# Hybrid decoder step: the sample batches' state products as pairs of 64-column strips of the array

## The chip, the cores and the metric

The kernel runs on one core of one Trainium2 chip. The metric is the device time of one execution in microseconds (us). The kernel before took 877.75 us, the median of three runs (877.45 to 877.9).

## The reference, cut to what matters

One decoder layer runs over 1024 prompt tokens and 8 sample batches of 8 tokens each: a combined projection, a pooling mixer beside a gated linear attention, an output projection, and a mixture of 16 experts. The change is in one output, the new attention state of the sample batches. For each batch b and head h (4 heads, 64 key and 128 value columns) the state is the decayed old state plus the sum over the batch's 8 tokens of key times value:

```python
S_new = jnp.exp(b_last[:, :, 0, :])[..., None] * S + jnp.einsum(
    'bhsk,bhsv->bhkv', ki * jnp.exp(b_last - bi), vi)
```

So 8 x 4 products of 64 x 128 are wanted, each over 8 tokens. The 64 sample tokens of all batches lie together on 64 partitions.

## The kernel before, in words

The program has three blocks, each ended by a barrier of all engines. `b1_all` computes the projections and the attention for the prompt and the samples. `b2_all` does the output projection, the residual, the second norm, the router, and the lists that say which rows go to which expert. `b3_all` walks through the experts, one step for each, with TensorE (PE) nearly always busy. In each block every engine has its own program, written out by hand, and works through it in that order; semaphores join them.

In `b1_all` the samples' decayed keys (`keys8`, 64 tokens x 256) and values (`v8`, 64 x 512) are left in SBUF, with `bmask` (64 x 8), which is 1 where a token belongs to a batch.

In `b2_all` the output projection goes through 9 row tiles (8 of 128 prompt rows, one of the 64 sample rows) and two column halves. The second half's loop (L1380 to L1404) has other work between its matmuls: after the third of the eight k it issues the transposes of the tile before (`turn`, L1351) and its router products (`logits`, L1377), later `partial_logits` (L1365). VectorE (DVE) has, for each tile i of that half, in this order (L1586 to L1605): the low parts of the next tile (`tile_lo`, L1545 and L1547), a router result (L1532), the reciprocal of the norm (L1594), the scaled row block `h2` = x times norm times weight (L1595, two whole operands from SBUF, 128 x 1024), the copy of the strip sums (`strips_out`, L1540), and the residual (L1563), which PE's next `turn` waits for.

GpSimd (POOL) waits until the last `tile_lo` has read the room `uT` (semaphore `r_al`, L1283). Then one multiply (L1284) writes `samples.masked` into that room: for each of the 8 batches the 256 keys of all 64 tokens, with the tokens of other batches set to zero. Its next instructions (L1287 on) wait for the router.

When the last sample tile is through, PE makes the state products (`states`, L1410). One batch b is two matmuls (L88), one for each pair p of heads: the masked keys of the pair (64 tokens x 128) are the weights and 256 value columns of the pair stream. That gives 128 x 256 in PSUM, of which two 64 x 128 blocks are wanted; the other two blocks pair one head's keys with the other head's values. ScalarE (ACT) takes the two wanted blocks out with two copies for each batch (`state_products_out`, L96) into `samples.added`, in the room `gT`. Each matmul has float32 operands and shows as two records in the trace, each with its own weight load. PE's order is: batches 0 to 2; the ranks (L1422 to L1428), for which it waits on DVE's choice of experts; batch 3; the lists of the first expert's rows, in two parts (L1438, c = 0 and 1), each after a DVE comparison (L1659); batches 4 to 7. From batch 4 on, a batch waits until its bank has been copied out. ACT copies batches 0 to 2, does two exponentials for the router, and copies batches 3 to 7. DVE meanwhile computes the choice of experts and the lists; after the first list (L1671 to L1675) POOL gathers the first expert's rows (L1297), and DVE goes on with the other lists and weights until L1700.

`samples.added` is read only in the last expert step (L2155), where DVE adds it to `S0`, the decayed old state.

`b3_all` begins on PE with reading the number of steps, the transposes of the gathered rows (L1900, L1905), the list products (L1893) and the gate and up matmuls (L1912).

Of the kernel before, what the change touches and what calls it, by code (L numbers as in the profile page):

```python
# [22 lines left out]
P = 128  # L23
# [3 lines left out]
DEC_B, DEC_T = 8, 8  # L27
NS = DEC_B * DEC_T
# [13 lines left out]
DK, DV = 64, 128  # L42
# [33 lines left out]
class Samples:  # L76


    def __init__(self, keys8, v8, o_dec, bmask, uT, gT):
        self.keys8, self.v8, self.o_dec, self.bmask = keys8, v8, o_dec, bmask  # L80
        self.masked = uT[0:NS, :, :].rearrange("p m t -> p (m t)")[:, 0:DEC_B * 256].rearrange("p (b d) -> p b d", b=DEC_B)
        self.added = gT[:].rearrange("p m t -> p (m t)")[:, 0:DEC_B * 2 * DV].rearrange("p (b q x) -> p b q x", b=DEC_B, q=2)


def state_products(nc, samples, bank, b, signal):

    for p in range(2):
        m = nc.tensor.matmul(bank[b % 4][:, p * 256:(p + 1) * 256], samples.masked[:, b, p * P:(p + 1) * P],  # L88
                             samples.v8[:, p * 256:(p + 1) * 256], start=True, stop=True)
    m.then_inc(signal, 1)  # L90


def state_products_out(nc, samples, bank, b, signal):

    for a in range(2):
        x = nc.scalar.copy(samples.added[64 * a:64 * a + 64, b, :, :],  # L96
                           bank[b % 4][64 * a:64 * a + 64, :].rearrange("p (q x) -> p q x", q=2)[:, :, a * DV:(a + 1) * DV])
    x.then_inc(signal, 1)

# [1095 lines left out]
def b2_all(nc, A, O, S0, Sp, s_w, samples, halves, sb, sem, e_w, wdn, bank, ident, onesf, eps_c, uT, gT, ring, x1, x_rows, h2_dram,  # L1195
# [41 lines left out]
    r_km, r_ku, r_us, r_ex = sem("r_km"), sem("r_ku"), sem("r_us"), sem("r_ex")  # L1237
# [15 lines left out]
    def _(pool):  # L1253
# [23 lines left out]
        for p in range(2):  # L1277
# [5 lines left out]
        pool.wait_ge(r_al, 2 * TT - 1 - PROJECTED)  # L1283
        nc.gpsimd.tensor_tensor(samples.masked, samples.keys8[:, :].unsqueeze(1).broadcast_to([NS, DEC_B, 256]),  # L1284
                                samples.bmask[:].unsqueeze(2).broadcast_to([NS, DEC_B, 256]), ALU.mult).then_inc(r_km, 1)
        pool.wait_ge(r_exd, 2)
# [56 lines left out]
    def _(pe):  # L1343
# [36 lines left out]
        for n in range(PROJECTED, 2 * TT):  # L1380
            h, i = n // TT, n % TT
# [6 lines left out]
            for k in range(KC):  # L1388
# [12 lines left out]
                m = nc.tensor.matmul(out, alo[:, s, k, 0:r], whi[:, k, :], start=False, stop=k == KC - 1)  # L1401
# [7 lines left out]

        def states(b):  # L1410
            if b == 2:
                pe.wait_ge(r_ssq, TT + 1)
            elif b >= 4:
                pe.wait_ge(r_us, b - 3)
            state_products(nc, samples, bank, b, r_ku)

        pe.wait_ge(r_x1, 2 * TT)
        pe.wait_ge(r_km, 1)
        for b in range(3):
            states(b)  # L1420
        pe.wait_ge(r_m, 1)
        nc.tensor.matmul(bank[7][:, 0:TT * NE], before[:], Mb[:].rearrange("p t e -> p (t e)"), start=True, stop=False)  # L1422
        for t in range(TT - 1):
            m = nc.tensor.matmul(bank[7][:, (t + 1) * NE:TT * NE].rearrange("p (t e) -> p t e", e=NE), onesb[:],
                                 Mb[:, t:t + 1, :].broadcast_to([P, TT - 1 - t, NE]), start=False, stop=t == TT - 2)
        m.then_inc(r_rk, 1)
        for t in range(TT):
            m = nc.tensor.matmul(bank[6][:, 0:NE], onesb[:], Mb[:, t, :], start=t == 0, stop=t == TT - 1)  # L1428
        m.then_inc(r_rk, 1)

        states(3)
        for c in range(2):
# [4 lines left out]
            for t in range(TT):  # L1437
                m = nc.tensor.matmul(bank[5][:, 2 * c:2 * c + 2], rows_0.oh[:, t, c * P:(c + 1) * P], table[:, 0, t, 0:2],  # L1438
                                     start=t == 0, stop=t == TT - 1)
        m.then_inc(rows_0.e_ix0, 1)  # L1440
        for b in range(4, DEC_B):
            states(b)

    @blk.scalar
    def _(act):
# [59 lines left out]

        def states_out(b):
            act.wait_ge(r_ku, b + 1)
            state_products_out(nc, samples, bank, b, r_us)

        for b in range(3):  # L1510
            states_out(b)
        act.wait_ge(r_exd, 1)
        nc.scalar.activation(t4[:], t4[:], ACT.Exp).then_inc(r_ex, 1)
        act.wait_ge(r_exd, 2)
        nc.scalar.activation(s2[:], s2[:], ACT.Exp).then_inc(r_ex, 1)
        for b in range(3, DEC_B):
            states_out(b)

# [744 lines left out]
```

## Time and profile before

| | |
|---|---|
| three runs | 877.45, 877.75 and 877.9 us |
| the profiled execution, first to last instruction | 877.9 us |
| PE, matmuls | 845.3 us busy (96%), 5828 records |
| PE, weight loads | 749.4 us (85%) |
| DVE | 526.8 us (60%) |
| ACT | 383.5 us (44%) |
| POOL | 244.6 us (28%), 272 instructions |
| the chain that ended last, by engine | PE 47%, other parts 1% or less each |
| state products (L88) | 32 records, from 409.1 to 426.4 us |
| their copies (L96) | 16, from 410.3 to 427.1 us |
| the masking multiply (L1284) | 1, 3.60 us, from 395.2 us |

The profile is of one execution. Its span is its own time as far as the device shows it, and 0.15 us more than the median of the three runs. The chain that ended last is followed back from the last instruction; its engine shares are of the whole span. What one stage is worth has to be read from the stretch from 395 to 430 us, where the second block ends and the third begins.

### The profile page before, as it was taken

How to read it: one execution, taken by the hardware profiler on the slowest of the kernel's cores; microseconds unless marked ns; L12 is line 12 of the kernel's file. 1: busy time of each engine (PE TensorE's matmuls, PEld its weight loads, DVE VectorE, ACT ScalarE, POOL GpSimd, SP SyncE). 2: the span in 40 equal slices, each digit the busy share in tenths (PEclk: the TensorE clock that was granted, in tenths of full speed). 3: DMA queues.
4: the chain of work that ended last, by engine and by line, in shares of the span. 5: the costliest groups of instructions: out<-in, count | busy, mean ns of one | idle time of the engine just before them, and what ended most of it. 6: DMA issues, size and time to landing. Idle time of an engine off the chain costs nothing.

```text
span 877.9 us, 15841 instructions
## 1 busy us (share of the span) xinstructions
PE 845.3 (96%) x5828; PEld 749.4 (85%) x5828; DVE 526.8 (60%) x1237; ACT 383.5 (44%) x734; POOL 244.6 (28%) x272
## 2 busy tenths in 40 slices
PE   6999999999999999998899999999999999999993
PEld 5989879999988787775789988889988999888992
DVE  5537424657778435557585676656666656766573
ACT  7545303656367425544334434344343444433442
POOL 1000000000000110002045654447545555445472
PEclk9999999999999999999599999999999999999997
DMA  9121001102222182336188889978899887898871
GB/s 291 43 97 47 2 0 49 49 1 56 49 96 96 59 274 91 150 145 216 60 275 290 300 304 325 306 271 310 291 310 324 307 288 278 290 360 295 286 256 50
DMA packets 118505, 166.56 MB, mean 190 GB/s; under 512 B 17012, under 2 KB 95928, under 8 KB 118469
## 3 DMA queue, kind: packets, MB, share of 16 engines
q1 hardware_dynamic: 103109, 135.48, 45.7%
q0 software_dynamic: 15360, 30.59, 10.2%
q8 instruction: 24, 0.39, 0.2%
q14 instruction: 12, 0.10, 0.0%
HBM read 146.84 MB, written 41.17 MB: 214 GB/s over the span
## 4 chain that ended last, share of the span: by engine, by line
PE 47%; another core or an unknown queue 1%; ACT 1%; issue 1%; DVE 0%; POOL 0%; ACTq 0%; POOLq 0%
PE bank L1912 31%; PE bank L1922 4%; PE bank L1933 3%; PE bank L1924 3%; PE bank L1923 3%; PE bank L1900 2%; PE bank L1893 1%; ACT split L2012 1%; POOL out L1820 0%; PE bank L1905 0%; DVE wdlo L2116 0%; PE bank L1939 0%; DVE x L2188 0%; ACT hs L2014 0%
## 5 line engine op out<-in xcount | busy, mean ns | idle before, releaser
L1912 PE MATMUL bank<-big,ring 128*128 128x160 f32 x2048 | 286.1, 301 | 0.1
L1912 PEld LDWEIGHTS bank<-big,ring 128*128 128x128 f32 x2048 | 281.9, 191 | 1.4
L1836 POOL TENSOR_TENSOR hold_at<-ident 128x1 f32<-128x1 f32 x63 | 53.1, 842 | 175.3 <-DVE lists L2083 128.4
L2116 DVE TENSOR_TENSOR wdlo<-wdn,split 128x1024 fp32r<-128x1024 f32 x64 | 76.7, 1219 | 0.0
L2008 ACT ACTIVATE sg<-bank 128x160 f32<-128x160 f32 x64 | 19.5, 304 | 109.7 <-PE bank L1912 95.4
L2012 ACT CAST split<-wdn 128x1024 fp32r<-128x1024 f32 x64 | 64.9, 1039 | 0.0
L502 PE MATMUL bank<-split,ring_r 128*128 128x384 f32 (+1 forms) x192 | 64.4, 336 | 0.1
L504 PE MATMUL bank<-split,ring_r 128*128 128x384 f32 (+1 forms) x192 | 61.7, 321 | 0.0
L2111 DVE TENSOR_TENSOR hs<-hid,hs 128x128 fp32r<-128x128 f32 x64 | 18.9, 295 | 57.3 <-ACT hs L2014 46.8
L1922 PE MATMUL bank<-split,hs 128*128 128x512 f32 x128 | 52.6, 411 | 0.0
L1399 PE MATMUL bank<-split,ring_r 128*128 128x512 f32 (+1 forms) x128 | 51.7, 404 | 0.3 <-PEq L1191 0.3
L1924 PE MATMUL bank<-split,hs 128*128 128x512 f32 x128 | 50.3, 393 | 0.0
L1923 PE MATMUL bank<-wdlo,hs 128*128 128x512 f32 x128 | 50.3, 393 | 0.0
L1400 PE MATMUL bank<-split,ring_r 128*128 128x512 f32 (+1 forms) x128 | 50.1, 392 | 0.0
L1401 PE MATMUL bank<-split,ring_r 128*128 128x512 f32 (+1 forms) x128 | 49.9, 390 | 0.0
L2017 ACT ACTIVATE squares<-z 128x256 f32<-128x256 f32 x16 | 6.7, 417 | 98.8 <-DVE z L2183 86.7
L2148 DVE TENSOR_TENSOR hid<-sg,bank 128x160 f32<-128x160 f32 x64 | 20.5, 320 | 48.1 <-ACT sg L2008 44.3
L1255 POOL MEMSET chunk<- 32x1 f32 x4 | 0.4, 92 | 169.7 <-POOLq L1191 169.5
L2050 DVE TENSOR_TENSOR big<-iota_w,rank_m 128x2304 bf16<-128x2304 f32 x17 | 43.5, 2560 | 0.0
L1820 POOL DMA_INDIRECT out<-ot,lists_now x32 | 37.6, 1174 | 10.0 <-issue 10.0
L502 PEld LDWEIGHTS bank<-split,ring_r 128*128 128x128 f32 x192 | 36.1, 188 | 0.9 <-ACT uT L713 0.3
L504 PEld LDWEIGHTS bank<-split,ring_r 128*128 128x128 f32 x192 | 36.0, 188 | 0.0
(390 smaller groups left out, 1788.4 us busy)
## 6 DMA issues: line engine op xcount, KB each, us to landing
wdn<-in_w_down SPq DMA_DIRECT2D x32, 1024.0 KB
ring<-in_w_gate SPq DMA_DIRECT2D x32, 1024.0 KB, 5.4
ring<-in_w_up SPq DMA_DIRECT2D x32, 1024.0 KB
ring<-in_w_in SPq DMA_DIRECT2D x8, 1024.0 KB, 5.9
x<-in_x_prompt SPq DMA_DIRECT2D x8, 512.0 KB, 6.1
h_rows<-h SPq DMA_DIRECT2D x8, 512.0 KB, 2.6
sums<-x SPq DMA_DIRECT2D x8, 512.0 KB, 3.6
v<-in_x_prompt SPq DMA_DIRECT2D x4, 512.0 KB, 5.4
```

Of the source, the lines that this page charges most:

```text
L502: nc.tensor.matmul(out, whi, hi[:, k, :], start=k == 0, stop=False)
L504: mm = nc.tensor.matmul(out, wlo, hi[:, k, :], start=False, stop=k == KC - 1)
L1399: nc.tensor.matmul(out, ahi[:, s, k, 0:r], whi[:, k, :], start=k == 0, stop=False)
L1400: nc.tensor.matmul(out, ahi[:, s, k, 0:r], wlo[:, k, :], start=False, stop=False)
L1401: m = nc.tensor.matmul(out, alo[:, s, k, 0:r], whi[:, k, :], start=False, stop=k == KC - 1)
L1836: nc.gpsimd.tensor_tensor(hold_at[:], ident[:, 0:1], ident[:, 1:2], ALU.add).then_inc(e_hold, 1)
L1912: x = nc.tensor.matmul(bank[f % 2][:, side * 256:side * 256 + W], ring[:, u, k, c0:c0 + P], xT[:, k, :], start=k == 0, stop=k == KC - 1)
L1922: nc.tensor.matmul(bank[2 + h][:, :], hi, whi, start=k == 0, stop=False)
L1923: nc.tensor.matmul(bank[2 + h][:, :], hi, wlo, start=False, stop=False)
L1924: x = nc.tensor.matmul(bank[2 + h][:, :], lo, whi, start=False, stop=k == 3)
L2012: nc.scalar.copy(wdhi[:, k, :], wdn[:, k // 2, (k % 2) * D:(k % 2 + 1) * D]).then_inc(e_wh, 1)
L2116: nc.vector.tensor_tensor(wdlo[:, k, :], wdn[:, k // 2, (k % 2) * D:(k % 2 + 1) * D], wdhi[:, k, :].bitcast(F32), ALU.subtract).then_inc(e ...
```

## The change

Each head's keys, unmasked, now become the weights (64 tokens x 64 columns), and the masked operand is the values: 8 batches x 512 columns. One matmul takes one head and four batches, so that 4 x 128 = 512 columns stream. The two heads of a pair write partitions 0 to 63 and 64 to 127 of the same bank: each uses one half of the array's columns. The index j = 0 to 3 counts pairs (p = j // 2) and groups of four batches. All of the 128 x 512 that a j leaves in PSUM is wanted, and one ACT copy takes it. Each j has its own bank, 0 to 3, so that the waits for copies (`r_us`) go.

The multiply on POOL is over 8 x 512 in place of 8 x 256 columns, and its result fills twice the room in `uT`. PE does j = 0 and 1 where it did batches 0 to 2, j = 2 where it did batch 3, and j = 3 where it did batches 4 to 7; ACT's copies move likewise. As `matmul` records are counted, 16 matmuls of 256 columns become 8 of 512.

```diff
--- before.py
+++ after.py
@@ -78,24 +78,24 @@
 
     def __init__(self, keys8, v8, o_dec, bmask, uT, gT):
         self.keys8, self.v8, self.o_dec, self.bmask = keys8, v8, o_dec, bmask
-        self.masked = uT[0:NS, :, :].rearrange("p m t -> p (m t)")[:, 0:DEC_B * 256].rearrange("p (b d) -> p b d", b=DEC_B)
+        self.masked = uT[0:NS, :, :].rearrange("p m t -> p (m t)")[:, 0:DEC_B * 512].rearrange("p (b d) -> p b d", b=DEC_B)
         self.added = gT[:].rearrange("p m t -> p (m t)")[:, 0:DEC_B * 2 * DV].rearrange("p (b q x) -> p b q x", b=DEC_B, q=2)
 
 
-def state_products(nc, samples, bank, b, signal):
-
-    for p in range(2):
-        m = nc.tensor.matmul(bank[b % 4][:, p * 256:(p + 1) * 256], samples.masked[:, b, p * P:(p + 1) * P],
-                             samples.v8[:, p * 256:(p + 1) * 256], start=True, stop=True)
+def state_products(nc, samples, bank, j, signal):
+
+    p, b0 = j // 2, j % 2 * 4
+    for a in range(2):
+        h = 2 * p + a
+        m = nc.tensor.matmul(bank[j][64 * a:64 * a + 64, :], samples.keys8[:, h * DK:(h + 1) * DK],
+                             samples.masked[:, b0:b0 + 4, h * DV:(h + 1) * DV], start=True, stop=True)
     m.then_inc(signal, 1)
 
 
-def state_products_out(nc, samples, bank, b, signal):
-
-    for a in range(2):
-        x = nc.scalar.copy(samples.added[64 * a:64 * a + 64, b, :, :],
-                           bank[b % 4][64 * a:64 * a + 64, :].rearrange("p (q x) -> p q x", q=2)[:, :, a * DV:(a + 1) * DV])
-    x.then_inc(signal, 1)
+def state_products_out(nc, samples, bank, j, signal):
+
+    p, b0 = j // 2, j % 2 * 4
+    nc.scalar.copy(samples.added[:, b0:b0 + 4, p, :], bank[j][:, :].rearrange("p (b x) -> p b x", b=4)).then_inc(signal, 1)
 
 
 class Halves:
@@ -1281,8 +1281,8 @@
         nc.gpsimd.memset(later[:, :, 3:4], 1.0).then_inc(r_fl, 1)
 
         pool.wait_ge(r_al, 2 * TT - 1 - PROJECTED)
-        nc.gpsimd.tensor_tensor(samples.masked, samples.keys8[:, :].unsqueeze(1).broadcast_to([NS, DEC_B, 256]),
-                                samples.bmask[:].unsqueeze(2).broadcast_to([NS, DEC_B, 256]), ALU.mult).then_inc(r_km, 1)
+        nc.gpsimd.tensor_tensor(samples.masked, samples.v8[:, :].unsqueeze(1).broadcast_to([NS, DEC_B, 512]),
+                                samples.bmask[:].unsqueeze(2).broadcast_to([NS, DEC_B, 512]), ALU.mult).then_inc(r_km, 1)
         pool.wait_ge(r_exd, 2)
         nc.gpsimd.tensor_copy(later[:, :, 1:2], both[:, :, 0:1]).then_inc(r_fl, 1)
         nc.gpsimd.tensor_tensor(later[:, :, 2:3], both[:, :, 0:1], both[:, :, 1:2], ALU.add).then_inc(r_fl, 1)
@@ -1407,17 +1407,15 @@
         partial_logits(TT - 1)
         logits(TT - 1)
 
-        def states(b):
-            if b == 2:
+        def states(j):
+            if j == 2:
                 pe.wait_ge(r_ssq, TT + 1)
-            elif b >= 4:
-                pe.wait_ge(r_us, b - 3)
-            state_products(nc, samples, bank, b, r_ku)
+            state_products(nc, samples, bank, j, r_ku)
 
         pe.wait_ge(r_x1, 2 * TT)
         pe.wait_ge(r_km, 1)
-        for b in range(3):
-            states(b)
+        for j in range(2):
+            states(j)
         pe.wait_ge(r_m, 1)
         nc.tensor.matmul(bank[7][:, 0:TT * NE], before[:], Mb[:].rearrange("p t e -> p (t e)"), start=True, stop=False)
         for t in range(TT - 1):
@@ -1428,7 +1426,7 @@
             m = nc.tensor.matmul(bank[6][:, 0:NE], onesb[:], Mb[:, t, :], start=t == 0, stop=t == TT - 1)
         m.then_inc(r_rk, 1)
 
-        states(3)
+        states(2)
         for c in range(2):
             if c == 0:
                 pe.wait_ge(r_m, 2)
@@ -1438,8 +1436,7 @@
                 m = nc.tensor.matmul(bank[5][:, 2 * c:2 * c + 2], rows_0.oh[:, t, c * P:(c + 1) * P], table[:, 0, t, 0:2],
                                      start=t == 0, stop=t == TT - 1)
         m.then_inc(rows_0.e_ix0, 1)
-        for b in range(4, DEC_B):
-            states(b)
+        states(3)
 
     @blk.scalar
     def _(act):
@@ -1503,18 +1500,18 @@
         act.wait_ge(r_half, 2)
         nc.scalar.activation(h2[0:NS, i % 2, :], h2[0:NS, i % 2, :], ACT.Copy, scale=rstd[0:NS, i:i + 1]).then_inc(r_h2, 1)
 
-        def states_out(b):
-            act.wait_ge(r_ku, b + 1)
-            state_products_out(nc, samples, bank, b, r_us)
-
-        for b in range(3):
-            states_out(b)
+        def states_out(j):
+            act.wait_ge(r_ku, j + 1)
+            state_products_out(nc, samples, bank, j, r_us)
+
+        for j in range(2):
+            states_out(j)
         act.wait_ge(r_exd, 1)
         nc.scalar.activation(t4[:], t4[:], ACT.Exp).then_inc(r_ex, 1)
         act.wait_ge(r_exd, 2)
         nc.scalar.activation(s2[:], s2[:], ACT.Exp).then_inc(r_ex, 1)
-        for b in range(3, DEC_B):
-            states_out(b)
+        for j in range(2, 4):
+            states_out(j)
 
     @blk.vector
     def _(dve):
```

On PE, in `b2_all` from the last router product of the samples to the end of the block (L88 and L90 are the state products, L1438 and L1436 the lists):

```order
L1377 MATMUL bank<-es,big 64x20
L88 MATMUL bank<-v,uT 128x256 x6
L1422 MATMUL bank<-Mb,before 128x144
...
L1428 MATMUL bank<-Mb,onesb 128x16 x9
L88 MATMUL bank<-v,uT 128x256 x2
L1438 MATMUL bank<-table,big 128x2 x18
L88 MATMUL bank<-v,uT 128x256 x8
L1702 UNCONDITIONAL_BRANCH
```

```order
L1377 MATMUL bank<-es,big 64x20
L90 MATMUL bank<-uT,keys 64x512 x4
L1420 MATMUL bank<-Mb,before 128x144
...
L1426 MATMUL bank<-Mb,onesb 128x16 x9
L90 MATMUL bank<-uT,keys 64x512 x2
L1436 MATMUL bank<-table,big 128x2 x18
L90 MATMUL bank<-uT,keys 64x512 x2
L1699 UNCONDITIONAL_BRANCH
```

Six, two and eight matmuls of 256 columns became four, two and two of 512; nothing else moved on PE.

On POOL, in `b2_all` from the clearing of `later` to the first gather, before and changed:

```order
L1281 MEMSET later 128x9
L1284 TENSOR_TENSOR uT<-keys,bmask 64x2048
L1287 COPY later<-both 128x9
L1288 TENSOR_TENSOR later<-both 128x9
L1290 CAST table<-later 128x9x16
L1297 DMA big<-h_rows,lists 128x1024
```

```order
L1281 MEMSET later 128x9
L1284 TENSOR_TENSOR uT<-v,bmask 64x4096
L1287 COPY later<-both 128x9
L1288 TENSOR_TENSOR later<-both 128x9
L1290 CAST table<-later 128x9x16
L1297 DMA big<-h_rows,lists 128x1024
```

The multiply has the same place and the same wait, and twice the elements.

## Rows read from the trace of the kernel before

**Rows 1.** The page's head and part 1: busy us, share, instructions.

```profile
span 877.9 us, 15841 instructions
PE 845.3 (96%) x5828; PEld 749.4 (85%) x5828; DVE 526.8 (60%) x1237; ACT 383.5 (44%) x734; POOL 244.6 (28%) x272
```

**Rows 2.** Chain that ended last, from 300 us: start, us, what.

```profile
429.00 1.98 PE bank L1900 x8
...
452.15 0.93 PE bank L1900 x8
...
453.30 1.86 PE bank L1933 x32
...
455.59 0.23 PE bank L1923
```

**Rows 3.** Timeline, second block's end: start, us, engine, line, tiles, shape [idle before].

```profile
425.12 0.41 DVE L1698 CAST table<-big 128x144 bf16<-128x144 f32 x1
426.38 0.75 ACT L96 COPY gT<-bank 64x256 f32<-64x256 f32 x2 [0.96 <-PE bank L88]
...
429.00 1.97 PE L1900 MATMUL bank<-ident,big 128*128 128x128 f32 x8 [2.66 <-issue]
...
430.15 0.59 ACT L1995 COPY big<-bank 128x512 f32<-128x512 f32 x1 [3.02 <-PE bank L1900]
```

**Rows 4.** Windows: length, busy PE, PEld, DVE, ACT, POOL (records), clock, DMA, GB/s.

```profile
426.00:426.50 0.50, 0.35 (x1) 0.00 (x0) 0.00 (x0) 0.12 (x1) 0.00 (x0) 0.50 0.00 0
```

**Rows 5.** Timeline, state products, their copies, ranks and lists.

```profile
409.09 2.85 PE L88 MATMUL bank<-v,uT 64*128 64x256 f32 x12
...
414.74 0.30 PE L1422 MATMUL bank<-Mb,before 128*128 128x144 bf16 x1 [2.79 <-DVE Mb L1641]
...
415.69 2.07 PE L88 MATMUL bank<-v,uT 64*128 64x256 f32 x4
...
417.69 0.40 PE L1438 MATMUL bank<-table,big 128*128 128x2 bf16 x9
...
418.82 0.40 PE L1438 MATMUL bank<-table,big 128*128 128x2 bf16 x9 [0.73 <-DVE big L1659]
...
419.16 7.19 PE L88 MATMUL bank<-v,uT 64*128 64x256 f32 x16
419.35 0.16 DVE L1671 TENSOR_SCALAR tok<-bank 128x2 f32<-128x2 f32 x1
...
421.25 0.19 DVE L1688 TENSOR_REDUCE big<-big 128x9 f32<-128x36 f32 x1
```

**Rows 6.** Timeline around the masking multiply, POOL, DVE and PE.

```profile
395.15 3.60 POOL L1284 TENSOR_TENSOR uT<-keys,bmask 64x2048 f32<-64x2048 f32 x1 [85.20 <-DVE ring_r L1547]
...
395.33 4.51 DVE L1595 SCALAR_TENSOR_TENSOR h<-x,rstd,g2b 128x1024 f32<-128x1024 f32 x1
...
399.96 0.67 DVE L1563 TENSOR_TENSOR x<-x,bank 128x512 f32<-128x512 f32 x1
...
400.45 0.40 PE L1401 MATMUL bank<-split,ring_r 128*64 128x512 f32 x1
...
400.68 0.42 PEld L1351 LDWEIGHTS bank<-ident,x 128*128 128x128 f32 x4 [0.33 <-DVE x L1563]
```

**Rows 7.** Groups of POOL by shape: busy us, mean ns, idle before.

```profile
L1278 POOL TENSOR_TENSOR S<-S,o_dec 128x1024 f32<-128x1024 f32 x2 | 3.8, 1892 | 0.0
L1284 POOL TENSOR_TENSOR uT<-keys,bmask 64x2048 f32<-64x2048 f32 x1 | 3.6, 3599 | 85.2 <-DVE ring_r L1547 85.2
```

**Rows 8.** Groups of DVE by shape, 340 to 395 us, same columns.

```profile
L1595 DVE SCALAR_TENSOR_TENSOR h<-x,rstd,g2b 128x1024 f32<-128x1024 f32 x6 | 7.7, 1285 | 0.2
```

**Rows 9.** Windows, columns as in rows 4: an idle stretch, two at half clock.

```profile
411.94:414.73 2.79, 0.01 (x1) 0.00 (x0) 2.41 (x15) 2.25 (x4) 0.00 (x0) 1.00 1.10 377
288.50:291.80 3.30, 3.00 (x7) 2.42 (x8) 2.58 (x4) 1.24 (x3) 0.00 (x0) 0.50 0.00 0
414.80:435.20 20.40, 16.95 (x96) 13.82 (x97) 13.35 (x51) 6.61 (x15) 3.36 (x5) 0.50 0.24 73
```

## The prediction

> **What bounds the kernel now.** I read the page first: PE's matmuls are busy 845.3 of 877.9 us [rows 1], and nearly all that the chain of waits names beside PE is small. So a change that moves 32 records and 16 copies can matter in two ways: it shifts the moment at which PE starts the experts, or it changes a wait of PE on the way there. For that I read the chain, then the timeline of the second block's end, then that of the stretch in which POOL's masking multiply runs, since that is the one instruction which the change makes longer.
>
> At the block's end the reader should see who is last at the barrier. DVE ends its lists at 425.12 + 0.41 = 425.53, ACT its last copy of state products at 426.38 + 0.75 = 427.13, and PE begins the experts at 429.00, 1.87 us after ACT [rows 3]. The state products decide the end: their last 16 records take 7.19 us from 419.16, at half the clock [rows 5, 9]. The gathered rows have landed earlier: the DMA engines do nothing in 426.00 to 426.50 [rows 4].
>
> At 395 us the reader should see DVE's scaled block (L1595) start at 395.33, 0.18 us after POOL's multiply, and last 4.51 us, where six others of the same shape took 1.285 us on average [rows 6, 8]. It ends at 399.84, 1.09 us after POOL ends at 395.15 + 3.60 = 398.75. DVE was held while POOL ran. Behind it stand the strip copy and the residual (L1563, 399.96 to 400.63), and PE's transposes (L1351) wait for that residual: their weight load starts at 400.68 after 0.33 us of idling that DVE's residual ended [rows 6]. So there is no slack left at this place: what lengthens POOL's multiply lengthens PE's wait.
>
> **The multiply, doubled.** POOL took 1.892 us for 1024 elements a partition and 3.599 for 2048 [rows 7], so 1.667 ns an element and 0.19 us fixed; 4096 elements take 7.01 us, 3.41 more. The multiply would end at 402.16, L1595 at 403.25, the residual at 404.04, and PE would wait from about 400.7 to 404.09. PE works through its program in order, so what stands behind the transposes (five k of the sample tile, its logits, the state products) is 3.41 later, and the router on DVE with it. Bounds: nothing, if DVE were held no longer than now, and 3.6, if the time just doubled. I take 3.41, from the two sizes. POOL's other work is covered: its next instruction follows the router, and PE wants the masked values only at 409.09 [rows 5], 6.9 us after 402.16 even before the shift.
>
> The Trainium skill, SBUF — State Buffer, section "SBUF: two separate sides", says that DVE, with two inputs from SBUF, and POOL take turns at a shared pair of ports, each for a whole instruction, and that the loser stands still. The trace shows nearly that, with 1.09 us after POOL's end in place of the whole 1.285; by the rule to the letter the stall would be some 0.2 us longer.
>
> **The state products and their copies.** A 256-column record took 2.85 / 12 = 0.24 us before the wait at 411.9 and 7.19 / 16 = 0.45 in the last run [rows 5]; a 512-column one is taken at twice that, 0.48 and 0.90. A j has two matmuls of two records. If the two strips pass together, a j takes 1.0 us at full and 1.8 at half clock, if one after the other 1.9 and 3.6. The trace has no 64-column strips side by side on 64 rows; nearest are the 32-column strips of L1933, of which 32 records of 256 columns took 1.86 us [rows 2] and not 32 x 0.24 = 7.7. I take "together".
>
> j = 0 and 1 fall ahead of PE's 2.79 us wait for the ranks [rows 5], which covers even the serial case (3.8 against 2.85 us). j = 2 takes 1.8 us where batch 3 took 2.07, so the lists (L1438 at 417.69 and 418.82) stay. j = 3 then runs from 419.16 to 421.0; a 128x512 copy took 0.59 us on ACT [rows 3], so ACT ends near 421.6, not 427.13. Late next is DVE at 425.53, as nothing in its lists depends on the later products. The barrier closes 427.13 - 425.53 = **1.60 us** earlier. That is the change's whole gain. Four copies replace 16, ACT is free for the exponentials no later than now, and DVE reads those only at 421.25 [rows 5].
>
> **The clock.** PE's granted clock is one of two levels, 2.4 or 1.2 GHz. It was at half from 414.8 to 435.2, after PE had stood idle from 411.94 to 414.73, 2.79 us [rows 9]. The new wait, some 3.4 us from 400.7, is longer, so I expect the clock to fall at about its end, while PE still has 15 projection matmuls, transposes and router products to do before the state products. A 512-column record there follows the next after 3.00 / 7 = 0.43 us at half clock [rows 9] and 0.23 at full [rows 2]. The price lies between nothing (no fall; no gain is possible, the clock being at full there now) and the rest of the block at half clock: 15 x 0.20 = 3.0 us, 1.98 - 0.93 = 1.05 for eight transpose records [rows 2], and by estimate 0.8 for eight half-size ones and the router, 4.85 together. The shortest stretch at half clock that I read in this trace is 288.50 to 291.80 [rows 9]; such a stretch, with 3.30 us of matmuls at 0.43 in place of 0.23, costs 1.5 us. I take 1.5: PE is dense again right after the wait, as it was in that stretch.
>
> **The sum.** 3.41 - 1.60 + 1.5 = 3.3 us. The profiled execution took 877.9 us, 0.15 more than the median; with that, 877.75 + 3.3 = 881.1 us.
>
> A last unknown is common to all cases: in the experts the clock rose at 435.2, 6.2 us after PE's start. If the rise did not move with a start some 1.8 us later, about half of that would be won back; if it moved further, as much could be lost. I allow 0.9 us to either side.
>
> **Rivals.**
> *No fall of the clock.* The stall comes, the clock holds. For it: the new wait is not far longer than the one of 2.79, and matmuls run up to its start. Against it: that shorter one was enough. 3.41 - 1.60 = +1.8 us, 879.6, or 878.7 to 880.5 by the rise in the experts.
> *The clock stays down until the block ends.* For it: from 414.8 on it stayed down 20 us although PE was busy for 16.95 us of them [rows 9]. Against it: the stretch at 288.5 rose again with dense matmuls. 3.41 - 1.60 + 4.85 = +6.7 us, 884.4.
> *The strips pass one after the other*, so that the change does not do what it says. j = 2 would take 3.6 us from 415.69 and end at 419.3; the lists would follow at 419.3 and 419.7 and end at 420.1, 0.9 later than the 419.22 of now, and DVE's L1671 behind them. j = 3 would end at 423.7, still ahead of DVE. With the likeliest clock +4.2 us, 882.0. Against it: the strips of L1933.
> *DVE goes first.* The place is the 0.18 us between the starts of POOL's multiply and DVE's L1595. If DVE's started first, POOL would be the one to wait, L1595 would take 1.285 us and PE's 0.33 us would vanish. The stall falls away with its clock, and -1.60 - 0.33 = -1.9 us leaves 875.8, faster. It decides as soon as POOL's start slips by more than 0.18 us. Against it: the change touches nothing ahead of either, and DVE has two small instructions to do between the event that releases POOL and L1595.
>
> **How the numbers follow.** Some 0.2%, 1.76 us here, can be told from no change. Chances: stall with a short stretch at half clock 0.35; stall without a fall 0.30; stall with the clock down to the block's end 0.22; strips one after the other, with any of these, 0.06; DVE first, or not held longer, 0.07. The first, second and fourth and most of the third lie within 878.6 (no fall, early rise in the experts) and 884.6; outside are the faster cases and the far end of the third. Faster: 0.07. Of the case without a fall, about half stays within 1.76 us, which with a little of the rest gives 0.17 for the same. Slower: 0.76.
>
> **What would show each step.** Right: the multiply with 64x4096 near 7.0 us; L1595 beside it near 7.9; an idle time of PE before L1351 of some 3.7 us in place of 0.33, released by DVE's residual; a granted clock of half in the microseconds after; the state products in 16 records, a j's two strips with the same start; DVE, not ACT, last before the barrier, and PE's start of the experts 1.87 us after it. Wrong: L1595 at its 1.3 us, or ended before the multiply, turns the sign. A clock of 1.00 up to the ranks takes 1.5 us off; one of 0.50 from 404 us to the experts adds 3.4.

## The result: slower by 0.4%, as forecast, with one term of the sum too large

The changed kernel takes 882.25 us, the median of 16 runs (881.19 to 883.73), against 878.32 us (877.23 to 882.6, 16 runs) for the kernel before. The ratio is 1.0041, with a 95% interval of 1.0031 to 1.0051, so 2.7 to 4.5 us more. The forecast was 881.1 us in a range of 878.6 to 884.6, from a sum of +3.3 us.

The page's head and part 1 of the changed kernel, which answer to [rows 1]:

```profile
span 879.6 us, 15797 instructions
PE 841.4 (96%) x5812; PEld 742.7 (84%) x5812; DVE 530.2 (60%) x1237; ACT 379.9 (43%) x722; POOL 248.7 (28%) x272
```

16 matmul records and 12 copies are gone. PE and ACT are busy 3.9 and 3.6 us less, DVE 3.4 and POOL 4.1 us more; the kernel is slower although its busiest engine is busy for less time.

The timeline of the changed kernel around the masking multiply, as [rows 6]. Its lines stand three below those of the kernel before: L1592 is the scaled block (L1595), L1560 the residual (L1563).

```profile
394.80 7.01 POOL L1284 TENSOR_TENSOR uT<-v,bmask 64x4096 f32<-64x4096 f32 x1 [85.21 <-DVE ring_r L1544]
394.97 7.92 DVE L1592 SCALAR_TENSOR_TENSOR h<-x,rstd,g2b 128x1024 f32<-128x1024 f32 x1
...
403.01 0.67 DVE L1560 TENSOR_TENSOR x<-x,bank 128x512 f32<-128x512 f32 x1
...
403.74 0.42 PEld L1351 LDWEIGHTS bank<-ident,x 128*128 128x128 f32 x4 [3.74 <-DVE x L1560]
```

POOL needs 7.01 us, DVE's scaled block is held until 402.89, 1.08 us after POOL's end at 401.81, and PE's weight loads for the transposes idle 3.74 us where they had idled 0.33. They start 8.94 us after the multiply's start, against 5.53 before [rows 6]: 3.41 us later. All of this is as the prediction has it to a few hundredths. This trace starts 0.35 us earlier than that of before (394.80 against 395.15), so distances below are counted from the multiply's start.

What the clock did, in windows of the changed kernel; columns as in [rows 4], the stretches as in [rows 9].

```profile
400.50:403.70 3.20, 0.00 (x0) 0.00 (x0) 3.19 (x3) 0.00 (x0) 1.31 (x1) 1.00 0.00 0
404.60:407.90 3.30, 3.30 (x12) 1.96 (x11) 2.26 (x5) 1.93 (x7) 0.00 (x0) 0.50 0.53 210
408.00:414.70 6.70, 5.12 (x56) 2.88 (x56) 3.02 (x10) 2.20 (x5) 0.00 (x0) 1.00 0.76 273
414.80:438.60 23.80, 12.89 (x87) 7.83 (x84) 17.07 (x71) 6.82 (x12) 3.37 (x5) 0.50 0.40 131
```

PE stands idle for 3.20 us at a granted clock of 1.00 (2.4 GHz); 0.9 us after it has started again the clock is at 0.50 (1.2 GHz) for one stretch of some 3.3 us, then at 1.00 up to 414.7, and at half again until 438.6. The third of the cases had it down to the block's end; that did not happen.

The second block's end in the timeline of the changed kernel, as [rows 3, 5]. L90 are the state products, L98 their copies, L1420 the ranks, L1436 the lists, L1668 the first instruction of DVE that takes a list, L1297 POOL's gathers, L1695 DVE's last instruction of the block, L2053 its first in the third, L1897 the experts' first transposes.

```profile
413.67 2.63 PE L90 MATMUL bank<-uT,keys 64*64 64x512 f32 x8
...
419.31 0.30 PE L1420 MATMUL bank<-Mb,before 128*128 128x144 bf16 x1 [3.00 <-DVE Mb L1638]
...
420.26 1.97 PE L90 MATMUL bank<-uT,keys 64*64 64x512 f32 x4
...
422.17 0.40 PE L1436 MATMUL bank<-table,big 128*128 128x2 bf16 x9
...
423.74 1.97 PE L90 MATMUL bank<-uT,keys 64*64 64x512 f32 x4
...
423.94 0.16 DVE L1668 TENSOR_SCALAR tok<-bank 128x2 f32<-128x2 f32 x1
...
425.76 0.59 ACT L98 COPY gT<-bank 128x512 f32<-128x512 f32 x1 [2.89 <-PE bank L90]
427.18 0.95 POOL L1297 DMA_INDIRECT big<-h_rows,lists  x1 [0.31 <-issue]
...
429.71 0.41 DVE L1695 CAST table<-big 128x144 bf16<-128x144 f32 x1
...
432.22 0.17 DVE L2053 TENSOR_SCALAR rank_m<-rank_m 128x9 f32<-128x9 f32 x1 [2.10 <-issue]
...
432.72 1.96 PE L1897 MATMUL bank<-ident,big 128*128 128x128 f32 x8 [7.01 <-issue]
```

Three things are to be seen. A j takes 1.97 us at half clock, near the 1.8 of two strips that run together and far from 3.6. ACT's last copy ends at 426.35, DVE's lists at 430.12: DVE is last, as forecast. But from the end of that last engine to PE's first transposes it is now 432.72 - 430.12 = 2.60 us, where it was 1.87 [rows 3]. DVE's list step L1668 is 29.14 us after the multiply's start, against 24.20 before [rows 5, 6]: 4.94 more, which is the 3.41 of the stall and 1.53 of the clock. PE's experts are 37.92 after it, against 33.85: 4.07 more.

The two profiled spans differ by only 1.7 us (879.6 and 877.9), less than the medians do. In the chain of the changed kernel the transposes of the second expert's rows, which are at 452.15 in [rows 2], are 3.58 us later:

```profile
455.73 0.94 PE bank L1897 x8
```

The difference between 3.58 and 1.7 us comes from stalls of PE that fell into the profiled execution of the kernel before and not into this one, as in these windows, of before and then of the changed kernel at the places that answer to them:

```profile
585.40:588.80 3.40, 2.54 (x40) 2.12 (x43) 1.64 (x4) 0.75 (x3) 1.97 (x1) 1.00 0.40 112
721.90:725.30 3.40, 2.39 (x39) 1.43 (x37) 3.04 (x6) 1.65 (x3) 0.00 (x0) 1.00 0.95 297
```

```profile
589.00:592.40 3.40, 3.40 (x60) 2.68 (x62) 3.04 (x7) 2.09 (x4) 0.92 (x1) 1.00 0.89 230
724.50:727.90 3.40, 3.40 (x44) 2.18 (x42) 2.53 (x12) 1.78 (x3) 0.00 (x0) 1.00 0.95 288
```

PE lost 0.86 and 1.01 us there before, nothing after; why it stalled there, no run shows. Spans of single executions differ by this much, so the medians of many runs decide how large the effect is, and the distances within the trace where it lies.

### The profile page after: what moved, and what is told of

The parts are those of the page before. It is cut to its first block and busy times, and to the rows that moved or that the text cites. A ratio compares the mean times of both kernels' runs of the same rounds, so it can differ in the third digit from the quotient of the medians.

```text
span 879.6 us, 15797 instructions
## 1 busy us (share of the span) xinstructions
PE 841.4 (96%) x5812; PEld 742.7 (84%) x5812; DVE 530.2 (60%) x1237; ACT 379.9 (43%) x722; POOL 248.7 (28%) x272
## 5 line engine op out<-in xcount | busy, mean ns | idle before, releaser
L502 PEld LDWEIGHTS bank<-split,ring_r 128*128 128x128 f32 x192 | 36.1, 188 | 0.9 <-ACT uT L713 0.3
```

The costliest lines, as they stand in the source:

```text
L502: nc.tensor.matmul(out, whi, hi[:, k, :], start=k == 0, stop=False)
```

## The experiments

The theory: the longer multiply holds DVE's scaled block, PE waits for it and loses some of its clock, and that costs more than the shorter tail brings back. A rival in each case is that one of these terms is something else. Five runs take a term out or put it in alone; the others go to the block's end, where the prediction's number was off. The first four (e1 to e4) share 29 runs of the kernel before with a median of 877.7 us, the next three (e5 to e7) 29 with 878.31.

### The multiply taken off POOL (e1)

In the changed kernel, ACT makes the masked values, one copy with a scale for each batch:

```diff
-        pool.wait_ge(r_al, 2 * TT - 1 - PROJECTED)
-        nc.gpsimd.tensor_tensor(samples.masked, ..., ALU.mult).then_inc(r_km, 1)
...
-        pe.wait_ge(r_km, 1)
+        pe.wait_ge(r_km, DEC_B)
...
+                if i == TT - 2:
+                    act.wait_ge(r_al, 2 * TT - 1 - PROJECTED)
+                    for b in range(DEC_B):
+                        nc.scalar.activation(samples.masked[:, b, :], samples.v8[:, :], ACT.Copy,
+                                             scale=samples.bmask[:, b:b + 1]).then_inc(r_km, 1)
                 act.wait_ge(r_x1, TT + i + 1)
```

> The changed kernel, but the masked values are written by eight ScalarE copies with a per-partition scale (64x512, one for each batch) in the microseconds in which ScalarE waits for the residual, and GpSimd does no multiply there. Theory (GpSimd's multiply holds VectorE's scaled block, and all the loss comes from that): the scaled block lasts 1.3 us, TensorE's idle time before the transposes L1351 is near 0 (the kernel before has 0.33, the changed one 3.25), the clock stays at full up to the ranks, and only the gain at the block's end is left: -0.33 - 0.87 = -1.2 us against the kernel before, 877.1 us on its median of 878.3. Rival (the new products themselves, or the change of the array's tiling, cost the time): still 3 to 4 us above the kernel before, 882.

Measured: 876.59 us (875.18 to 877.52, 12 runs) against 877.7, ratio 0.998 [0.997, 0.999]. The timeline of this kernel, ACT's copies and the scaled block (here L1594), and a window, columns as in [rows 4]:

```profile
396.23 5.02 ACT L1479 ACTIVATE uT<-v,bmask 64x512 f32<-64x512 f32 x8
...
396.42 1.28 DVE L1594 SCALAR_TENSOR_TENSOR h<-x,rstd,g2b 128x1024 f32<-128x1024 f32 x1
...
401.79 0.99 PE L1348 MATMUL bank<-ident,x 128*128 128x128 f32 x8
...
410.40:411.00 0.60, 0.60 (x4) 0.11 (x2) 0.53 (x3) 0.60 (x1) 0.00 (x0) 0.50 1.06 377
```

The scaled block takes 1.28 us with ACT's eight copies beside it, PE's matmuls have no idle time before the transposes, and the clock stays at 1.00 to 410.2. It does not stay up to the ranks, as was expected: from 410.4 it is at 0.50, and the first two j take 3.51 us in place of the 1.93 of the fourth experiment, where it is at 1.00. That costs nothing here, as PE waits for the ranks behind them: DVE's list step comes 24.19 us after ACT's first copy, and in the kernel before 24.20 after the multiply's start. So the loss of the change is the multiply on POOL, and not the strips; without it the kernel with the strips is faster than both.

The step of the prediction by which PE's 0.33 us of idling ahead of the transposes [rows 6] would vanish without the hold does not stand. Here the last projection matmul starts at 401.55, as the weight load of the transposes does, and the transposes follow 0.24 us later; in [rows 6] the last one starts at 400.45 and the weight load at 400.68, 0.23 later. The idling was of the weight loads alone, and there is nothing to win.

### The multiply lengthened, the products left alone (e2)

In the kernel before, keys and values lie in one tensor, and the multiply goes over 512 of its columns for each batch; the products read the first 256.

```diff
-        keys8 = sb("keys8", [NS, 256])
-        v8 = sb("v8", [NS, 512])
+        kv8 = sb("kv8", [NS, 768])
+        keys8, v8 = kv8[:, 0:256], kv8[:, 256:768]
...
+        samples.both8 = kv8[:, 0:512]
...
-        nc.gpsimd.tensor_tensor(samples.masked, samples.keys8[:, :].unsqueeze(1).broadcast_to([NS, DEC_B, 256]),
-                                samples.bmask[:].unsqueeze(2).broadcast_to([NS, DEC_B, 256]), ALU.mult).then_inc(r_km, 1)
+        nc.gpsimd.tensor_tensor(samples.masked, samples.both8.unsqueeze(1).broadcast_to([NS, DEC_B, 512]),
+                                samples.bmask[:].unsqueeze(2).broadcast_to([NS, DEC_B, 512]), ALU.mult).then_inc(r_km, 1)
```

> The kernel before, with GpSimd's masking multiply lengthened to 64x4096 (it also multiplies 256 value columns, which nothing reads); products and copies as before. Theory: the stall of 3.41 us and the short stretch at half clock (1.5 us) come with the multiply alone: the scaled block lasts 7.9 us, TensorE idles some 3.3 us before L1351, +4.9 us against the kernel before, 883.2 us. Rival (the loss comes from the new products): no change, 878.3 us.

Measured: 884.01 us (881.73 to 887.41, 6 runs), ratio 1.0067 [1.0044, 1.0089]. Timeline and window of this kernel:

```profile
396.31 7.01 POOL L1285 TENSOR_TENSOR uT<-kv,bmask 64x4096 f32<-64x4096 f32 x1 [85.22 <-DVE ring_r L1548]
396.49 7.92 DVE L1596 SCALAR_TENSOR_TENSOR h<-x,rstd,g2b 128x1024 f32<-128x1024 f32 x1
...
405.26 1.04 PE L1352 MATMUL bank<-ident,x 128*128 128x128 f32 x8 [3.25 <-DVE x L1564]
...
406.30:409.50 3.20, 3.20 (x10) 1.98 (x10) 2.25 (x5) 1.74 (x6) 0.00 (x0) 0.50 0.53 211
```

The hold is that of the changed kernel to 0.01 us, and the wait and the stretch at half clock are there again. From the multiply's start to the experts' transposes this trace has 38.84 us, 4.99 more than the kernel before. By the six runs it is 3.9 to 7.8 us, which holds the 4.99 but is too wide for the next step. The whole change has 4.07 more in its trace; so by the traces the strips and copies give back 4.99 - 4.07 = 0.92 us, not the 1.60 of the prediction.

### The wait filled, so that the clock holds (e3)

In the changed kernel, 13 matmuls whose result nobody uses stand in PE's wait:

```diff
                 if h == 1 and k == 3:
+                    if i == TT - 1:
+                        pe.wait_ge(r_x1, 2 * TT - 2)
+                        for _ in range(13):
+                            nc.tensor.matmul(bank[3][:, :], ahi[:, 0, 0, :], whi[:, 0, :], start=True, stop=True)
```

> The changed kernel, with 13 matmuls of 512 columns (3.0 us at full clock, into a bank that is free then; nothing reads their result) in TensorE's wait before the transposes L1351. The stall stays. Theory (the wait makes the clock fall, and the fall costs 1.5 us): granted clock 1.00 from the wait up to the ranks, the state products 1.5 us sooner behind the multiply's end, 880.7 us against the changed kernel's 882.25. Rival (the fall has another cause, or costs nothing on the way to the router): as the changed kernel, 882.2 us or a little more.

Measured: 880.01 us (878.8 to 881.59, 12 runs), ratio 1.0026 [1.0016, 1.0035], against 1.0041 for the change: some 1.3 us less, though the intervals just overlap. Timeline and window:

```profile
400.41 3.11 PE L1393 MATMUL bank<-split,ring_r 128*128 128x512 f32 x13
403.82 1.04 PE L1351 MATMUL bank<-ident,x 128*128 128x128 f32 x8 [0.31 <-DVE x L1564]
...
404.60:407.90 3.30, 3.30 (x32) 1.95 (x32) 2.26 (x5) 2.01 (x7) 0.00 (x0) 1.00 0.62 247
```

The same 3.30 us hold 32 records at a clock of 1.00, in place of 12 at 0.50. The end of DVE's lists comes 1.39 us sooner after the multiply's start (33.93 against 35.32). So the fall of the clock is its own term, of 1.4 to 1.5 us, and it does not come at this place when PE's wait is filled. The clock did not hold up to the ranks, as the theory had it: from 411.8 it is at 0.50, after stretches in which PE was busy for about half of the time, and the first two j take 3.68 us. As in the first experiment that lies ahead of the wait for the ranks, which is still 1.96 us long.

### The multiply in two halves (e4)

In the changed kernel, two instructions of four batches each:

```diff
-        nc.gpsimd.tensor_tensor(samples.masked, ..., ALU.mult).then_inc(r_km, 1)
+        for b in (0, 4):
+            nc.gpsimd.tensor_tensor(samples.masked[:, b:b + 4, :], ..., ALU.mult).then_inc(r_km, 1)
...
-        pe.wait_ge(r_km, 1)
+        pe.wait_ge(r_km, 2)
```

> The changed kernel, with GpSimd's multiply in two instructions of four batches each, one behind the other. Theory (the ports are held for one instruction, and VectorE's waiting instruction gets its turn between two): the scaled block lasts about 4.5 us as in the kernel before, TensorE idles 0.3 us, the clock does not fall before the ranks, and the block's end gains 0.87 us: 877.5 us. Rival (GpSimd's next instruction takes the ports again at once): the scaled block lasts 7.9 us and the time is that of the changed kernel, 882.2 us.

Measured: 877.55 us (876.11 to 880.67, 12 runs), ratio 0.9999 [0.9985, 1.0012]: the loss is gone. The 0.87 us of gain that the theory adds can neither be seen nor excluded in an interval of this width; in the trace the experts' transposes (428.76) come 33.07 us after the multiply's start, 0.78 sooner than before. Timeline and window:

```profile
395.69 8.13 POOL L1285 TENSOR_TENSOR uT<-v,bmask 64x2048 f32<-64x2048 f32 x2 [85.21 <-DVE ring_r L1545]
...
395.86 4.50 DVE L1593 SCALAR_TENSOR_TENSOR h<-x,rstd,g2b 128x1024 f32<-128x1024 f32 x1
...
401.23 1.04 PE L1352 MATMUL bank<-ident,x 128*128 128x128 f32 x8
...
402.98 1.93 DVE L1593 SCALAR_TENSOR_TENSOR h<-x,rstd,g2b 128x1024 f32<-128x1024 f32 x1
...
411.60:415.20 3.60, 0.00 (x0) 0.00 (x0) 3.12 (x17) 2.10 (x3) 0.00 (x0) 0.54 1.08 364
```

POOL needs 8.13 us for both, yet the scaled block is through after 4.50: it gets its turn between the two instructions, and POOL is the one that waits (8.13 - 2 x 3.60 = 0.93 us). The second half then holds the next scaled block for 0.65 us (1.93 in place of 1.28), which nobody waits for. What counts is the length of one POOL instruction, not their sum. The clock is at 1.00 until the first two j are through; the window is PE's wait for the ranks, which comes behind them. By the Trainium skill (SBUF — State Buffer, "SBUF: two separate sides") the engine that starts first keeps the pair for the whole instruction; this trace agrees, and shows beside it that the turn changes hands where that instruction ends.

### The masks on ACT without the strips (e6)

The kernel before with ACT copies as above, over the 256 columns of the keys:

```diff
-        nc.gpsimd.tensor_tensor(samples.masked, samples.keys8[:, :]..., ALU.mult).then_inc(r_km, 1)
...
+                    for b in range(DEC_B):
+                        nc.scalar.activation(samples.masked[:, b, :], samples.keys8[:, :], ACT.Copy,
+                                             scale=samples.bmask[:, b:b + 1]).then_inc(r_km, 1)
```

> The kernel before, products and copies as they are, with the masked keys written by eight ScalarE copies with a scale (64x256) and no multiply on GpSimd. Theory (the multiply costs the kernel before only the 0.33 us by which TensorE waits there): -0.3 us against the kernel before, 877.4 us, and the distance from the last ScalarE copy to the first transpose stays 1.87 us; the run with the masks on ScalarE and the new products is 0.9 us faster than this one. Rival (the products give nothing, the masks on ScalarE all of it): as fast as that run, 876.6 us.

Measured: 878.01 us (877.51 to 879.73, 11 runs) against 878.31, ratio 1.0000 [0.999, 1.001]. Timeline:

```profile
395.47 3.31 ACT L1482 ACTIVATE uT<-keys,bmask 64x256 f32<-64x256 f32 x8
...
395.66 1.29 DVE L1597 SCALAR_TENSOR_TENSOR h<-x,rstd,g2b 128x1024 f32<-128x1024 f32 x1
...
426.69 0.74 ACT L96 COPY gT<-bank 64x256 f32<-64x256 f32 x2 [0.96 <-PE bank L88]
...
428.80 0.17 DVE L2058 TENSOR_SCALAR rank_m<-rank_m 128x9 f32<-128x9 f32 x1 [2.96 <-issue]
```

The short hold of the kernel before cost it nothing that can be measured: the scaled block falls from 4.51 to 1.29 us and the time stays. This kernel and that of the first experiment differ by strips and copies, and by the width of ACT's mask copies: 1.0000 against 0.998. That is what the strips are worth, 1.8 us by the ratios with some 1.2 us to either side, and 0.8 by the medians, each against the runs of before beside it; by the traces 0.85 us at PE's first transposes, counted from ACT's first mask copy (32.98 and 33.83).

### What the block's end waits for (e5, e8)

The third block's first instruction of DVE marks the barrier without PE's own waits. Counted from the end of the engine that was last: 428.80 - 427.43 = 1.37 us where ACT is last (above), 432.22 - 430.12 = 2.10 in the changed kernel. In the windows of the changed kernel POOL's gathers, the only DMA in flight there, still run 0.4 us behind DVE's end. Before, they ran until 425.9, which is behind DVE's end at 425.53 as well, but 1.2 us ahead of ACT's [rows 3, 4]. The changed kernel first, then the kernel before:

```profile
430.40:430.50 0.10, 0.00 (x0) 0.00 (x0) 0.00 (x0) 0.00 (x0) 0.00 (x0) 0.50 0.01 0
430.50:431.00 0.50, 0.00 (x0) 0.00 (x0) 0.00 (x0) 0.00 (x0) 0.00 (x0) 0.50 0.00 0
```

```profile
425.80:425.90 0.10, 0.10 (x2) 0.00 (x0) 0.00 (x0) 0.00 (x0) 0.00 (x0) 0.50 0.02 0
```

So the theory here is that the barrier also waits until POOL's gathers have landed. Two kernels take gathers out of the second block, on top of the first experiment, by issuing them at the head of the third. One gather moved:

```diff
-        for dst, src, which, signal in ((rows_0.xg, h2_dram, 0, rows_0.e_xg), (rows_0.xg2, expert_rows(h2_dram), 1, rows_0.e_xl)):
+        for dst, src, which, signal in ((rows_0.xg, h2_dram, 0, rows_0.e_xg),):
...
+        nc.gpsimd.indirect_dma_start(
+            out=rows_0.xg2, out_offset=None, in_=expert_rows(h2_dram),
+            in_offset=bass.IndirectOffsetOnAxis(ap=rows_0.lists0[:, 1:2], axis=0)).then_inc(rows_0.e_xl, 16)
```

> The kernel of the run with the masks on ScalarE, with the second of the two first gathers (a quarter of each leftover row) issued at the start of the third block. In the changed kernel TensorE's first transpose comes 2.60 us after the end of VectorE's last list (430.12 to 432.72), where the kernel before has 1.87 us after ScalarE's last copy. Theory (the barrier also waits until GpSimd's gathers have landed, 0.5 to 0.7 us after VectorE is done, and this eats part of the 1.60 us): with the second gather out of the way the distance is 2.1 us. The time itself is then lost again, because the second gather lands late in the third block: 1 to 3 us above the run with the masks on ScalarE, 878 to 880 us. Rival (the distance is VectorE's own, from its last instruction to the barrier): it stays at 2.6 us.

Measured: 879.22 us (877.46 to 879.66, 10 runs), ratio 1.0008 [0.9999, 1.0017]. Both gathers moved, the loop of the diff above as a whole:

> The kernel of e5_late_second_gather with the first expert's first gather at the head of the third block too, so that POOL has no gather under way when the second block ends. In e1 the last list (VectorE's cast) ended at 426.61 and VectorE's first instruction of the third block began at 428.71, 2.10 us later; in e5, with one gather still ahead of the end, 426.67 to 428.41, 1.74 us. In the kernel before, where ScalarE's copy ended last, it was 427.13 to 428.50, 1.37 us. Theory (the block's end waits for POOL's gathers to land): the distance is 1.37 us, give or take 0.1. Rival (the block's end is simply longer after VectorE than after ScalarE, and e5's shorter distance has another cause): 1.74 or more. Under both PE then waits for the first gather, which now starts after the barrier: its transposes begin some 3 to 4 us later than in e1, and the time is 879 to 882 us; that delay is the edit's own and decides nothing.

Measured: one run, 880.42 us beside 878.2. The timelines of the two, first with one gather moved (and the last window in which the DMA engines are busy), then with both:

```profile
426.26 0.41 DVE L1697 CAST table<-big 128x144 bf16<-128x144 f32 x1
...
426.60:426.70 0.10, 0.00 (x0) 0.00 (x0) 0.07 (x1) 0.00 (x0) 0.00 (x0) 0.50 0.01 0
...
428.41 0.17 DVE L2058 TENSOR_SCALAR rank_m<-rank_m 128x9 f32<-128x9 f32 x1 [1.74 <-issue]
...
432.63 0.69 PE L1907 MATMUL bank<-ident,big 128*128 128x128 f32 x2 [1.73 <-DMA big<-h_rows,lists]
```

```profile
425.46 0.41 DVE L1693 CAST table<-big 128x144 bf16<-128x144 f32 x1
427.48 0.17 DVE L2055 TENSOR_SCALAR rank_m<-rank_m 128x9 f32<-128x9 f32 x1 [1.61 <-issue]
...
432.96 1.97 PE L1899 MATMUL bank<-ident,big 128*128 128x128 f32 x8 [11.50 <-DMA big<-h_rows,lists]
```

From DVE's last cast to the marker it is 2.10 us with two gathers ahead of the end, 1.74 with one, 1.61 with none. To PE's first transposes it is 2.27 us with one gather moved (428.94), between the theory's 2.1 and the rival's 2.6. With both moved, the theory's 1.37 is not reached, and the rival's 1.74 is undercut.

What settles it is a distance that no expectation named. With windows of 0.1 us the end of the DMA engines' last work can be read in every kernel in which ACT is done early and a gather is ahead of the barrier, and the marker is set beside it (DVE is the last engine, but for e7, where unused matmuls of PE end 0.3 us behind it):

| kernel | DMA ends | marker | after the DMA's end | after DVE's end |
|---|---|---|---|---|
| changed | 430.5 | 432.22 | 1.72 | 2.10 |
| e1 | 427.0 | 428.71 | 1.71 | 2.10 |
| e3 | 429.3 | 431.01 | 1.71 | 2.20 |
| e4 | 426.5 | 428.26 | 1.76 | 2.17 |
| e5 | 426.7 | 428.41 | 1.71 | 1.74 |
| e7 | 426.6 | 428.31 | 1.71 | 2.23 |

The distance from DVE varies by 0.49 us, that from the end of the gathers by 0.05. So the barrier waits for POOL's gathers to land, and in the changed kernel they are last at it, not DVE. Of the 0.73 us by which the end has grown, 0.49 go with the gathers. The 0.24 that would be left without them (1.61 after DVE, 1.37 after ACT) stay open: the barrier seems to take longer after DVE than after ACT, but that rests on one execution, and no run shows why. The moves are no gain, since PE then waits for the gathers themselves (L1907, L1899).

### The gap at the end filled (e7)

On top of the first experiment, 11 unused matmuls behind the last state product, to bring the clock back before the experts:

```diff
         states(3)
+        for _ in range(11):
+            nc.tensor.matmul(bank[4][:, :], whi[:, 0, 0:P], whi[:, 1, :], start=True, stop=True)
```

> The kernel of the run with the masks on ScalarE, with 11 matmuls of 512 columns (nothing reads their result) behind the last state product, where TensorE now idles 7.0 us up to the experts. In that run the clock is at half from 410.4 to 434.3 us, 5.1 us into the experts. Theory (a denser end of the block brings the clock back earlier): the rise comes before or within 2 us of the first transposes, and half of the time by which it comes earlier is won: 1.5 to 2.5 us below the run with the masks on ScalarE, 874.1 to 875.1 us. Rival (the fillers end too early, and the clock is judged again by the idling behind them): the rise stays some 5 us behind the first transposes, 876.6 us; if they make TensorE the last at the barrier, up to 0.5 us more.

Measured: 875.98 us (874.71 to 879.21, 12 runs), ratio 0.9979 [0.9967, 0.999], not to be told from 0.998 without them (2.3 us below the kernel before by the medians, where the first experiment has 1.1, with some 1 us to either side of each). The windows show why:

```profile
421.60:426.30 4.70, 4.70 (x13) 3.43 (x11) 4.03 (x14) 0.59 (x1) 2.15 (x2) 0.54 0.44 140
426.40:428.80 2.40, 0.00 (x0) 0.01 (x1) 0.45 (x4) 0.00 (x0) 0.00 (x0) 1.00 0.00 0
...
429.40:432.60 3.20, 3.14 (x30) 2.99 (x29) 1.25 (x10) 2.54 (x4) 0.00 (x0) 0.50 0.60 188
```

The clock does come back, at the end of the matmuls, and stands at 1.00 through the 2.40 us in which PE waits for the barrier; then it falls once more, half a microsecond after the experts have begun. In the experts it is at 0.50 for 3.3 us and up again 3.8 us behind the first transposes, later than the theory's 2 and sooner than the rival's 5. But in e4, whose end is not filled, it is up 3.5 us behind them. So no gain of the matmuls is shown.

## Why the prediction was right, and which step was off

- **The multiply.** 7.01 us were worked out from two sizes, 7.01 were measured. The hold of the scaled block until 1.09 us after POOL (1.08 measured) and the 3.41 us of PE's stall hold as well; lengthening the multiply alone reproduces them. That DVE goes first, the rival on the faster side, fell: it started 0.17 us behind POOL, nearly as before (0.18).
- **The clock.** The short stretch at half clock was forecast with 3.30 us and a price of 1.5; the granted clock was 0.50 in the 3.30 us from 404.6, and the price was 1.53 by the list step and 1.39 by the run with the wait filled. The rivals of no fall and of a clock that stays down fell with it. The 3.30 us were taken over from one other stretch of the trace, and no run shows why this one is as long; that they agree so closely is luck as far as is known. The rise in the experts moved along with PE's start, to 5.9 us behind it for 6.2 before, so the allowance of 0.9 us was hardly used.
- **The strips.** They run together, with 1.97 us a j at half clock for the 1.8 forecast, and 1.93 for two at full clock in e4 for 1.0 each. DVE, and not ACT, is the last engine before the barrier, as forecast.
- **The step that was off** is the term of 1.60 us for the tail, "The barrier closes 427.13 - 425.53 = 1.60 us earlier". It measured 0.87: 35.32 - 30.38 = 4.94 us of delay at DVE's end, but only 4.07 at PE's transposes. The step took for granted that the 1.87 us between the last engine and PE stay, and that the gathers do not matter because they had landed by 426. Ahead of ACT's end they had; but they had landed 0.4 us after DVE's, at 425.9, and the window that the prediction read, 426.00 to 426.50, begins behind that. Gathers and lists moved together with the later router, so with the end moved up to DVE's the gathers were last. The prediction wrote "Late next is DVE" and named one engine, where POOL's gathers were later. With the 1.71 us that the barrier takes behind them in the other traces, the marker of the kernel before could have come at 425.9 + 1.71 = 427.61 in place of 428.50, by this estimate a gain of 0.89 us, close to the 0.87 measured. Without any gather 0.24 of the missing 0.73 us would still be lost, and why is open.
- **The sum** with the measured terms is 3.41 + 1.53 - 0.87 = 4.07 us; the medians differ by 3.93. Of the 1.15 us between 882.25 and 881.1, 0.57 is the kernel before, whose median over 16 runs is 878.32 and not 877.75. The rest, 0.6, is the tail's 0.73, less what trace and medians differ by.
- **The base.** The prediction took the span of 877.9 us for the profiled execution's own time. The device time of the changed kernel's profiled execution is 881.32 with a span of 879.6, 1.7 more, and other runs show the same (877.34 and 875.6 in the first experiment). By estimate the profiled execution of before took some 879.6 us, 1.3 above the median, which fits the two stalls seen in it. As only differences were added to the median, the forecast did not suffer.

## What to carry to other kernels

Before giving POOL a longer instruction, look at what DVE runs beside it and who waits for that: the cost here was not POOL's time but a single DVE instruction held for all of it, and cutting POOL's instruction in two, or giving it to ACT, took the cost away. A gain at the end of a block is not the distance to the next engine alone; transfers that were hidden behind the old end are candidates too, and their landing has to be read against the new end, not the old one. And a wait of PE is to be priced with the clock that follows it.

## What the hardware showed that was not expected

- A DVE instruction held by POOL gets its turn between two POOL instructions that follow each other directly: 4.50 us of hold with two of 3.60 us, 7.92 with one of 7.01.
- DVE's scaled block next to ACT's eight copies over the operands of POOL's multiply ran its 1.28 us: these copies did not hold it.
- The block's end came 1.71 to 1.76 us after the landing of POOL's gathers in six kernels, whatever DVE's last instruction did (1.74 to 2.23).
- After a gap of PE the granted clock did not fall at one place: it fell after PE had started again in the changed kernel (from 404.6) and in that with the filled end (from 429.4, after a gap of 2.40 us at 1.00), but inside the gap before the ranks in e4 (0.54 in 411.6 to 415.2).
- It also fell without such a gap: in e1 from 410.4 and in e3 from 411.8, where PE had worked on and off. Kernels with the same instructions up to there, such as e1 and e7, differ in this, so one trace does not settle such a fall.
